# A two-block transformer kernel on one Trainium2 core: inputs by features from the host, a gate's columns on VectorE, eight convolution taps as products on ScalarE

## The chip, the cores and the metric

The kernel runs on one core of one Trainium2 chip. The metric is the device time of one execution, in microseconds (us). The time before is the median of 3 runs, 733.89 us (733.76 to 734.76). A profile is one execution, recorded by the hardware. TensorE (PE; PEld is its weight load) multiplies, VectorE (DVE), ScalarE (ACT) and GpSimd (POOL) work on rows of 128 partitions, SyncE (SP) queues the weight transfers.

## What is computed

Two transformer blocks over 256 positions of 1024 features, in float32, one after the other. Only the first block is touched by the change.

```
silu_c, silu_cc = silu(c), silu(c_ctx)
sh1, sc1, g1, sh2, sc2, g2 = split(silu_c @ w_ada + b_ada)        # and csh1, csc1 for c_ctx
hx = rms_norm(x, norm1_g) * (1 + sc1) + sh1
hc = rms_norm(ctx, norm1_g) * (1 + csc1) + csh1
q, k, v, u = split_proj(hx @ w_in);  kc, vc = hc @ w_in[:, 512:1536]
attn = softmax([rope(q) rope(k)^T / 8 + bias, q kc^T / 8]) [v, vc]   # 8 heads
conv = silu(layer_norm(depthwise_conv(a * sigmoid(b), 31 taps) + bias))
x = x + g1 * ([attn, conv] @ w_out)
x = x + g2 * (square(relu(modulated_norm(x) @ w_mlp1)) @ w_mlp2)
```

## The kernel before

Every engine has a program written out by hand, an instruction queue in fixed order; the engines meet by semaphores (`S[...]`), and a wait stops everything behind it on its engine. A large product is made of three in the type fp32r: each weight unit (1 MB, four or eight blocks of 128 rows) is split by ScalarE into a high half (`WH`, line 1004) and by VectorE into the rest (`WL`, line 1481), each activation likewise (`AH`/`AL`, `CH`/`CL`), and `part` multiplies high by high, high by low, low by high (lines 414 to 416). SP loads the units in the order of `weight_units` into a ring of six slots, each as soon as the unit before it in the slot has been used. The unsplit modulation weights may take either half of a slot.

The stages of the first block, with their place in the profile:

1. Start (0 to 17 us). x arrives by rows. ScalarE sums its squares, GpSimd takes the power -0.5, VectorE scales x (`hat`). TensorE multiplies filler (`keep_busy`, line 476).
2. First loop (to 51 us). For each of eight feature blocks, `mod_first` (line 454) makes 256 columns of shift and scale, as 32 rows in four groups, `mod_turn` turns them to features (line 468) together with the block of scaled x (line 465), VectorE sums and modulates, and `ab` multiplies by the convolution's 1024 input columns (lines 490 to 496).
3. Projections (to 109 us): k, then k and v of the context, q, v. The scaled context is transposed by `c_turn` in the middle of k. VectorE rotates k and q (`rope1`) and adds the taps of the convolution (`taps`, line 1496, one instruction for one tap of one of four channel blocks); ScalarE copies results out of the banks and makes the first tap.
4. Softmax (to 157 us): eight units of two heads and one half of the positions. For each unit TensorE does the scores of the next, half a product of the modulation (`mod_second`, line 433), the tail of the last one (`mod_second_tail`: transposes for shift and scale, for a gate a product with a column of ones, line 621, that spreads the sum to all rows), the values of the unit before (`pv1`, line 598), the other half, and the transposes of the probabilities (`turn1`, line 396). VectorE finds the maxima (`soft1`), scales, and does the remaining taps in between.
5. The output product, the norm, and the feed forward (199 to 340 us) in eight chunks `c`: `up_wide` (lines 731 to 734) and `down1`.

Of the kernel before, what the change touches and what calls it, by code (L numbers as in the profile page):

```python
# [11 lines left out]
D = 1024  # L12
# [12 lines left out]
class Mem:  # L25


    def __init__(self, nc, ctx):
# [42 lines left out]
        self.XC2 = M("XC2", 56, [128, 2, D])  # L71
# [8 lines left out]
        self.cacc = M("cacc", 72, [128, 4, 256])  # L80
        self.ccen = M("ccen", 28, [128, 4, 256])
# [18 lines left out]
        self.combR = M("combR", 84.75, [128, 1], F32R)  # L100
        self.hid = [M(f"hid{i}", 32 + 4 * i, [128, 2, 512]) for i in range(2)]
# [37 lines left out]
l_out w_hi w_lo eps ones silu_c csp hp_zero  # L139
sq_sum mean_sq rstd ada1_mm rows1_dve rows1_turned mod1_sum mod1  # L140
x_hat mx_dve mx_act kx c_hat c_turned mc_dve mc_act kc
a_mm b_mm gate_u u u_turned hp conv_first conv k_mm q_mm v_mm k_out kc_out q_out v_out vc_out rope_mul kr qr qk_turned qk_act
comb_r ada2_mm rows2 rows2_lo rows2_turned mod2_sum mod2
bias_zero scores1 max1 exp1 rl1 p1_norm p1_norm_act p1_turned pt1 pv1
conv_pair conv_block conv_sums conv_dve conv_act conv_rs k_conv a2
out_mm o1_hi o1_lo res1 nscale_dve nscale_act n_turned n_dve n_act kn
m1_mm m1_up m2_mm mlp_sum mlp_act hid_turned hid_hi hid_lo btw
# [3 lines left out]
scores2 max2 exp2 rl2 p2_norm pr2_turned pt2 pv2 g_out g_sig  # L151
y_hi y_lo up_mm merge mrg_turned mrg_hi mrg_lo
out2_mm res2 gu_mm dn_mm silu_g hid2 res3 last_sum x_g y_out y_act""".split()
# [27 lines left out]

OUT_ORDER = [(2, 0), (3, 0), (0, 0), (1, 0), (2, 1), (3, 1), (0, 1), (1, 1)]
# [11 lines left out]
def weight_units(d, S):  # L194
# [27 lines left out]
    for n in range(16):  # L222
        i, half = n // 2, n % 2
        c0 = (3072, 3584, 4096, 4608, 2048, 2560, 5120, 5632)[i]
        add(("ada2", i), "w_ada", 4 * half, 4, [("w_ada", c0, 512)], False, ("ada2_mm", n + 1))
        if n == 7:
            out(2)
            out(3)
        if n == 11:
            out(0)  # L230
            out(1)
# [34 lines left out]
    slots += [2, 12, 3, 13, 4, 14, 5, 15, 0, 1, 2, 12, 3, 13, 4, 5, 2, 12, 3, 13]  # L266
    while len(slots) < len(units):
        slots.append((2, 3, 0, 1, 4, 5)[(len(slots) - 42) % 6])
# [16 lines left out]
def sync_program(e, m, S, units, out, d):  # L285
    w = Waits(e)

# [8 lines left out]
    for tb in range(2):  # L296
        e.dma_start(m.X[:, tb, :], d["x"][128 * tb:128 * tb + 128, :]).then_inc(S[f"l_x{tb}"], 16)
# [3 lines left out]
    for n in range(14, len(units)):  # L301
        load(n)
    for n in range(3):
# [6 lines left out]
def pool_program(e, m, S, d):  # L310
    w = Waits(e)

    def power(i):

        w.wait_ge(S["eps"], 2)
# [18 lines left out]
    e.memset(m.ones[:, :], 1.0).then_inc(S["ones"], 1)  # L334
# [8 lines left out]
    e.memset(m.hp[:, :, 0:15], 0.0).then_inc(S["hp_zero"], 1)  # L343
    e.memset(m.hp[:, :, 271:288], 0.0).then_inc(S["hp_zero"], 1)
# [4 lines left out]
    w.wait_ge(S["eps"], 2)  # L349
# [16 lines left out]
def tensor_program(e, m, S, by):  # L366
# [58 lines left out]
    def mod_unit(unit, k0, bk, sem):  # L425
# [4 lines left out]
        w.wait_ge(S["csp"], 2)  # L430
# [14 lines left out]
    def mod_first(e8):  # L445
# [4 lines left out]
        w.wait_ge(S["csp"], 2)  # L450
# [8 lines left out]
    def mod_turn(e8):  # L459
# [3 lines left out]
        w.wait_ge(S["x_hat"], 2)  # L463
        for tb in range(2):
            e.transpose(bank[b][:, 256 + tb * 128:384 + tb * 128], m.S1[:, tb, 128 * e8:128 * e8 + 128], m.ident[:, :])
# [4 lines left out]
        frees(b, ("mx_dve", e8 + 1))  # L470

    def keep_busy(count):

        w.wait_ge(S["ones"], 1)
# [24 lines left out]
    keep_busy(11)  # L499
    mod_first(0)  # L500
    mod_turn(0)
    keep_busy(8)
    for e8 in range(8):
# [3 lines left out]
        if e8 < 7:  # L507
            mod_turn(e8 + 1)
        ab(e8, 1)
    for tb in range(2):  # L510
        frees(tb, ("u", tb + 1))
        frees(2 + tb, ("gate_u", tb + 1))

    def c_turn(i):
        w.wait_ge(S["c_hat"], 2)
        b = turn(pair(m.XC2, 2 * i), "c_turned")
        frees(b, ("mc_act", 3 * i - 1) if i else ("mc_dve", 2))
# [5 lines left out]

    def c_turns(i):
        c_turn(i)
        c_turn(i + 1)
# [9 lines left out]
    product(by["k"], m.AH, m.AL, 0, 4, "k_mm", x_ready, 512, lambda: c_turns(0))  # L536
    frees(4, ("k_out", 1))
    c_turns(2)
# [23 lines left out]
    qk_turn(m.KR, 2, "kr", 1)  # L562
    qk_turn(m.QR, 3, "qr", 1)
# [46 lines left out]
    def mod_second_tail(i):  # L610
# [6 lines left out]
        else:  # L617
            w.wait_ge(S["comb_r"], 1)
# [1658 lines left out]
```

## Time and profile before

| | us |
|---|---|
| median of 3 runs | 733.89 |
| lowest, highest | 733.76, 734.76 |
| profiled execution, its own time | 736.95 |
| span of its instructions | 735.1 |
| TensorE busy | 722.5 (98%) |
| TensorE weight loads busy | 577.7 (79%) |
| VectorE busy | 508.5 (69%) |
| ScalarE busy | 397.8 (54%) |
| GpSimd busy | 24.9 (3%) |

An instruction's duration runs from its start to its result, and the next one may start before that; so the price of an instruction in a full queue is the step from its start to the start of the next. Busy shares count overlapping instructions once. In the windows below stand, in this order, the stretch and its length, the busy time (and number of instructions) of PE, PEld, DVE, ACT and POOL, TensorE's granted clock as a share of 2.4 GHz, the busy share of the DMA engines, and GB/s; in the timelines the start, the time until the last result, engine, line, operation, output and inputs, and the idle time before it, if any.

### The profile page before, as it was taken

How to read it: one execution, taken by the hardware profiler on the slowest of the kernel's cores; microseconds unless marked ns; L12 is line 12 of the kernel's file. 1: busy time of each engine (PE TensorE's matmuls, PEld its weight loads, DVE VectorE, ACT ScalarE, POOL GpSimd, SP SyncE). 2: the span in 40 equal slices, each digit the busy share in tenths (PEclk: the TensorE clock that was granted, in tenths of full speed). 3: DMA queues.
4: the chain of work that ended last, by engine and by line, in shares of the span. 5: the costliest groups of instructions: out<-in, count | busy, mean ns of one | idle time of the engine just before them, and what ended most of it. 6: DMA issues, size and time to landing. Idle time of an engine off the chain costs nothing.

```text
span 735.1 us, 9749 instructions
## 1 busy us (share of the span) xinstructions
PE 722.5 (98%) x3806; PEld 577.7 (79%) x3806; DVE 508.5 (69%) x924; ACT 397.8 (54%) x662; POOL 24.9 (3%) x44
## 2 busy tenths in 40 slices
PE   7999999999999999999999999999999999999996
PEld 5668885568888888888878777778888888888885
DVE  3688999889667555565988799865857445544544
ACT  3366336886666545556545677666466344434432
POOL 1020011000100000000010000000000000000000
PEclk8999999999999999999999999999999999999999
DMA  9984939954464656545528533344366655655511
GB/s 366 385 325 172 364 114 357 370 171 165 162 221 167 229 182 215 172 157 190 160 96 302 203 116 115 118 171 170 115 230 203 197 173 189 206 177 171 173 58 57
DMA packets 73741, 144.90 MB, mean 197 GB/s; under 512 B 4112, under 2 KB 27664, under 8 KB 72672
## 3 DMA queue, kind: packets, MB, share of 16 engines
q1 hardware_dynamic: 71888, 138.98, 54.6%
q0 software_dynamic: 1520, 5.03, 1.9%
q8 instruction: 30, 0.49, 0.3%
q10 hardware_dynamic: 288, 0.27, 0.1%
q14 instruction: 15, 0.12, 0.0%
HBM read 143.22 MB, written 1.05 MB: 196 GB/s over the span
## 4 chain that ended last, share of the span: by engine, by line
PE 92%; DVE 3%; issue 2%; DMA 1%; ACT 1%; POOL 0%; SPq 0%; POOLq 0%; DVEq 0%
PE bank L414 22%; PE bank L416 22%; PE bank L415 22%; PE bank L734 5%; PE bank L396 5%; PE bank L732 3%; PE bank L433 2%; PE bank L454 1%; DMA W<-in_w_ada 1%; PE bank L576 1%; PE bank L490 1%; PE bank L598 1%; PE bank L851 1%; PE bank L873 1%; DVE WL L1481 1%
## 5 line engine op out<-in xcount | busy, mean ns | idle before, releaser
L1481 DVE TENSOR_TENSOR WL<-W,WH 128x1024 fp32r<-128x1024 f32 (+2 forms) x222 | 249.5, 1169 | 47.7 <-ACT WH L1004 47.4
L1004 ACT ACTIVATE WH<-W 128x1024 fp32r<-128x1024 f32 (+2 forms) x222 | 211.5, 1011 | 52.8 <-DMA W<-in_w_mlp 40.3
L414 PE MATMUL bank<-WH,AHL 128*128 128x512 f32 (+1 forms) x480 | 189.2, 394 | 0.3 <-DVE AHL L1490 0.3
L416 PE MATMUL bank<-WH,AHL 128*128 128x512 f32 (+1 forms) x480 | 185.4, 386 | 0.0
L415 PE MATMUL bank<-WL,AHL 128*128 128x512 f32 (+1 forms) x480 | 185.2, 386 | 0.0
L414 PEld LDWEIGHTS bank<-WH,AHL 128*128 128x128 f32 x480 | 90.2, 188 | 21.5 <-issue 3.2
L416 PEld LDWEIGHTS bank<-WH,AHL 128*128 128x128 f32 x480 | 90.2, 188 | 18.7
L415 PEld LDWEIGHTS bank<-WL,AHL 128*128 128x128 f32 x480 | 90.3, 188 | 16.9
L414 PE MATMUL bank<-WH,HH 128*128 128x512 f32 (+1 forms) x218 | 84.9, 390 | 0.0
L416 PE MATMUL bank<-WH,HL 128*128 128x512 f32 (+1 forms) x218 | 84.5, 388 | 0.0
L415 PE MATMUL bank<-WL,HH 128*128 128x512 f32 (+1 forms) x218 | 84.4, 387 | 0.0
L734 PE MATMUL bank<-AHL,WH 128*128 128x512 f32 x168 | 60.5, 398 | 0.0
L732 PE MATMUL bank<-AHL,WL 128*128 128x256 f32 x192 | 50.0, 281 | 0.0
L1496 DVE SCALAR_TENSOR_TENSOR cacc<-hp,vec,cacc 128x256 f32<-128x256 f32 x120 | 48.3, 475 | 0.0
L416 PEld LDWEIGHTS bank<-WH,HL 128*128 128x128 f32 x218 | 40.9, 188 | 8.5
L415 PEld LDWEIGHTS bank<-WL,HH 128*128 128x128 f32 x218 | 41.0, 188 | 8.3
L414 PEld LDWEIGHTS bank<-WH,HH 128*128 128x128 f32 x218 | 40.9, 188 | 8.0
L1413 ACT ACTIVATE rel<-bank 128x256 f32<-128x256 f32 x22 | 8.5, 384 | 62.2 <-PE bank L416 61.1
L1490 DVE TENSOR_TENSOR hid<-bank,rel 128x256 f32<-128x256 f32 x22 | 9.3, 424 | 42.2 <-ACT rel L1413 42.2
L732 PEld LDWEIGHTS bank<-AHL,WL 128*128 128x128 f32 x192 | 36.3, 189 | 2.0
L734 PEld LDWEIGHTS bank<-AHL,WH 128*128 128x128 f32 x168 | 31.6, 188 | 6.7
L1784 DVE TENSOR_TENSOR HL<-bank,HH 128x256 fp32r<-128x256 f32 (+1 forms) x26 | 11.1, 460 | 30.9 <-ACT HH L1012 30.9
(265 smaller groups left out, 829.5 us busy)
## 6 DMA issues: line engine op xcount, KB each, us to landing
W<-in_w_mlp SPq DMA_DIRECT2D x32, 1024.0 KB, 5.4
W<-in_w_in SPq DMA_DIRECT2D x24, 1024.0 KB, 5.1
W<-in_w_ada SPq DMA_DIRECT2D x12, 1024.0 KB, 7.5
WX<-in_w_ada SPq DMA_DIRECT2D x12, 1024.0 KB, 9.4
W<-in_w_gate SPq DMA_DIRECT2D x22, 512.0 KB, 4.1
W<-in_w_up SPq DMA_DIRECT2D x22, 512.0 KB, 5.3
W<-in_w_down SPq DMA_DIRECT2D x11, 1024.0 KB, 4.9
W<-in_w_out SPq DMA_DIRECT2D x8, 1024.0 KB, 5.0
```

The costliest lines, as they stand in the source:

```text
L396: ins = e.transpose(bank[b][:, c * 128:c * 128 + 128], src, m.ident[:, :])
L414: e.matmul(po, hs, wh[:, k, c0:c0 + cw], start=first and k == 0, stop=False)
L415: e.matmul(po, hs, wl[:, k, c0:c0 + cw], start=False, stop=False)
L416: ins = e.matmul(po, ls, wh[:, k, c0:c0 + cw], start=False, stop=last and k == unit.nk - 1)
L433: ins = e.matmul(bank[bk][32 * g:32 * g + 32, :], m.csp[:, k0 + g, :], wv[:, g, :], start=k0 == 0, stop=k0 == 4, tile_position=(0, 32 * g))
L732: ins = e.matmul(bank[4 + j][:, 0:256], wl[:, k, js], m.AH[:, 4 * i + k, :], start=False, stop=False)
L734: ins = e.matmul(both, wh[:, k, js], m.AHL[:, :, 4 * i + k, :], start=False, stop=i == 1 and k == 3)
L1004: e.activation(m.WH[unit.slot][:, c], m.W32[unit.slot][:, c], ACT.Copy).then_inc(S["w_hi"], 1)
L1481: e.tensor_tensor(m.WL[unit.slot][:, c], m.W32[unit.slot][:, c], m.WH[unit.slot][:, c].bitcast(F32), ALU.subtract).then_inc(S["w_lo"], 1)
L1490: e.tensor_tensor(o, a, b, op).then_inc(S[sem], 1)
L1496: e.scalar_tensor_tensor(o, a, scalar, b, op0, op1).then_inc(S[sem], 1)
L1784: e.tensor_tensor(L[:, k0:k0 + nj, ts], bank[b][:, 0:nj * 128].rearrange("p (j n) -> p j n", j=nj), H[:, k0:k0 + nj, ts].bitcast(F32), ALU ...
```

## The change

- The host also gives x and the context by features (`xt`, `ctxt`). x is no longer scaled and transposed: ScalarE squares it by features, TensorE sums the squares over features with a column of ones (`x_sums`), and the inverse root is spread over all partitions as a row (`spread`), copied to `rB`; VectorE multiplies x by the scale and `rB`, ScalarE adds the shift while it takes the high half, VectorE adds it again while it takes the low one. x by rows is loaded later, for the residual. The context by rows is still loaded for its squares; VectorE multiplies `CT` by the spread root in two instructions; its transposes go.
- The start has 6 + 4 + 4 filler products instead of 11 + 8.
- The gate g2 (columns 5120 to 6144) is no longer a product of the softmax stage. Its weights are loaded to `GW` in the feed forward, in four transfers behind the second unit of `m2` of chunks 2 to 5; VectorE adds them row by row (`gate_rows`, eight instructions of 1024 columns), and TensorE sums over the partitions (`gate_sum`) in chunk 6.
- The last eight of 31 taps: ScalarE multiplies (`tap_products`, 32 instructions of 256 columns), VectorE adds all four channel blocks at once (`add_product`, eight of 1024). VectorE's own taps fall from 120 to 88.
- ScalarE's copy of V to its place waits for the last of these sums, since V shares memory with the products. Some semaphores are merged.

```diff
@@ sync_program
-    for tb in range(2):
-        e.dma_start(m.X[:, tb, :], d["x"][128 * tb:128 * tb + 128, :]).then_inc(S[f"l_x{tb}"], 16)
+    for h in range(2):
+        e.dma_start(m.XT[:, 4 * h:4 * h + 4, :], d["xt"][:, 4 * h:4 * h + 4, :]).then_inc(S[f"l_x{h}"], 16)
...
     for n in range(14, len(units)):
+        if n == 16:
+            e.dma_start(m.CT[:, :, :], d["ctxt"]).then_inc(S["l_ct"], 16)
+        if n == 22:
+            e.dma_start(m.X[:, :, :], d["x"].rearrange("(t p) n -> p t n", p=128)).then_inc(S["l_x"], 16)
         load(n)
+        if n in gate_at:
+            gate_rows(gate_at.index(n))
@@ tensor_program
+    def x_sums():
+
+        for h in range(2):
+            w.wait_ge(S["sq_sum"], h + 1)
+            for k in range(4 * h, 4 * h + 4):
+                for tb in range(2):
+                    ins = e.matmul(bank[6 + tb][:, 0:1], m.xsq[:, k, tb * 128:tb * 128 + 128], m.ones[:, 0:1], start=k == 0,
+                                   stop=k == 7)
+        ins.then_inc(S["r_mm"], 1)
+
+    def spread(b, i):
+
+        w.wait_ge(S["l_id"], 16)
+        w.wait_ge(S["rstd"], i + 2)
+        for tb in range(2):
+            ins = e.matmul(bank[b][:, tb * 128:tb * 128 + 128], m.stat[:, 40 + i + tb:41 + i + tb].to_broadcast([128, 128]),
+                           m.ident[:, :], start=True, stop=True)
+        ins.then_inc(S["r_mm"], 1)
...
-    keep_busy(11)
+    keep_busy(6)
+    x_sums()
+    keep_busy(4)
+    spread(turn_bank("x_spread", 6), 0)
+    frees(6, ("setup", 5))
     mod_first(0)
     mod_turn(0)
-    keep_busy(8)
+    keep_busy(4)
...
-        mod_second(2 * u)
-        if u:
-            mod_second_tail(u - 1)
+        if u < 4:
+            mod_second(2 * u)
+        if u in (1, 2, 3, 4, 6):
+            mod_second_tail(min(u - 1, 4))
...
-        mod_second(2 * u + 1)
+        mod_second(2 * u + 1 if u < 4 else u + 4)
...
+    def gate_sum():
+
+        w.wait_ge(S["comb_r"], 2)
+        w.wait_ge(S["g2_hi"], 1)
+        w.wait_ge(S["g2"], 9)
+        for n in range(2):
...
+            e.matmul(bank[4 + n][:, :], m.onesR[:, :].to_broadcast([128, 128]), m.gH[:, cs], start=True, stop=False)
+            e.matmul(bank[4 + n][:, :], m.onesR[:, :].to_broadcast([128, 128]), m.gL[:, cs], start=False,
+                     stop=True).then_inc(S["g2_mm"], 1)
@@ scalar_program
+    tap_products(0, 1)
     for tb in range(2):
         from_bank("k_mm", 6 + 2 * tb, m.KC[:, tb, :], tb, slice(0, 512), "kc_out")
+        if tb == 0:
+            tap_products(2)
     hi(2)
+    tap_products(3)
     for tb in range(2):
         from_bank("q_mm", 2 + 2 * tb, m.Q[:, tb, :], 2 + tb, slice(0, 512), "q_out", 0.125)
+    tap_products(4, 5)
...
     for tb in range(2):
         from_bank("v_mm", 2 * tb + 2, m.VC[:, tb, :], 4 + tb, slice(0, 512), "vc_out")
+        if tb == 0:
+            tap_products(6, 7)
     qk_features(0, m.kcT)
     qk_features(1, m.qT)
+    w.wait_ge(S["conv_add"], CONV_PRODUCTS)
     from_bank("v_mm", 6, m.V[:, 0, :], 0, slice(0, 512), "v_out")
@@ vector_program
-            hat(m.XC, m.XC2, 0, 2, "c_hat")
-    lo()
-    mean_square(3, (3,))
-    hat(m.XC, m.XC2, 1, 3, "c_hat")
-    lo()
+            mean_square(3, (3,))
+    lo(2)
...
+    for i in range(2):
+        cv = m.CT[:, 4 * i:4 * i + 4, :]
+        rv = bank[m.turn_bank["c_spread", 1]][:, 0:256]
+        tt(cv, cv, rv.unsqueeze(1).to_broadcast([128, 4, 256]), ALU.mult, "c_hat")
     modulate_c0()
...
-    rope1(m.KR, m.Kt, "kr")
-    taps(20)
+    rope1(m.KR, m.Kt, "rotated")
+    taps(8)
+    add_product()
+    add_product()
+    taps(8)
     lo(2)
-    taps(8)
+    add_product()
+    taps(4)
+    add_product()
     w.wait_ge(S["q_out"], 2)
-    w.wait_ge(S["kr"], 1)
-    rope1(m.QR, m.Q, "qr")
-    taps(52)
+    w.wait_ge(S["rotated"], 1)
+    rope1(m.QR, m.Q, "rotated")
+    for n in range(4):
+        taps(6 if n else 2)
+        add_product()
+    taps(16)
...
+        if c < 6:
+            gate_rows(2 * c - 4)
+            gate_rows(2 * c - 3)
+        else:
+            gate_add()
```

## Rows read from the trace of the kernel before

**Rows 1.** The page's head and its first section, TensorE: busy us (share) and instructions

```profile
span 735.1 us, 9749 instructions
...
PE 722.5 (98%) x3806; PEld 577.7 (79%) x3806; DVE 508.5 (69%) x924; ACT 397.8 (54%) x662; POOL 24.9 (3%) x44
```

**Rows 2.** Waits of TensorE: line, waited for: us in total, times, longest

```profile
PE bank L468 <- DVE rows L1521: 0.4, 1, 0.4
...
PE bank L433 <- DVE rows2L L1490: 0.2, 1, 0.2
```

**Rows 3.** Windows: busy us by engine, granted clock, DMA share, GB/s

```profile
9.50:16.00 6.50, 6.42 (x36) 4.78 (x36) 3.00 (x8) 2.72 (x5) 0.00 (x0) 0.51 1.01 419
...
36.00:42.00 6.00, 6.00 (x43) 4.31 (x42) 3.58 (x12) 3.54 (x7) 0.00 (x0) 1.00 0.98 388
120.00:140.00 20.00, 19.97 (x188) 11.08 (x184) 19.75 (x63) 16.72 (x38) 3.02 (x5) 1.00 1.05 379
```

**Rows 4.** Timeline of the start: start, us, engine, line, op, tiles, shape, idle before

```profile
5.42 1.04 ACT L1016 ACTIVATE S<-X 128x1024 f32<-128x1024 f32 x1
...
7.34 0.55 POOL L317 TENSOR_TENSOR stat<-stat 128x1 f32<-128x1 f32 x1 [0.93 <-DVE stat L1507]
7.93 0.75 DVE L1493 TENSOR_SCALAR S<-X,stat 128x1024 f32<-128x1024 f32 x1 [0.67 <-POOL stat L317]
...
9.57 1.94 PE L454 MATMUL bank<-W,csp 128*32 128x256 f32 x16 [2.72 <-DMA W<-in_w_ada]
...
12.53 3.56 PE L476 MATMUL bank<-ones 128*128 128x128 f32 x16
...
15.04 0.42 DVE L1490 TENSOR_TENSOR AHL<-S,AHL 128x256 fp32r<-128x256 f32 x1
...
17.02 0.73 PE L490 MATMUL bank<-WH,AHL 128*128 128x512 f32 x2
```

**Rows 5.** Timeline of the softmax stage, units 6 and 7

```profile
148.97 0.49 DVE L1493 TENSOR_SCALAR s<-s,rl 128x512 f32<-128x512 f32 x1
...
149.72 1.06 PE L433 MATMUL bank<-WX,csp 128*32 128x512 f32 x8
...
150.71 1.34 PE L396 MATMUL bank<-ident,s 128*128 128x128 f32 x8
...
152.05 1.07 ACT L1012 ACTIVATE PT<-bank 128x512 f32<-128x512 f32 x2
...
155.90 0.61 PE L639 MATMUL bank<-ones,csum 128*128 128x1 f32 x4
...
156.37 1.07 PE L396 MATMUL bank<-ident,s 128*128 128x128 f32 x8
```

**Rows 6.** Timeline of TensorE around the first transposes of the context

```profile
53.45 0.39 PE L416 MATMUL bank<-WH,AHL 128*128 128x512 f32 x1
53.68 1.03 PE L396 MATMUL bank<-ident,XC 128*128 128x128 f32 x8
...
54.79 0.39 PE L415 MATMUL bank<-WL,AHL 128*128 128x512 f32 x1
```

**Rows 7.** Timelines of ScalarE and of VectorE, projections of the first block

```profile
47.76 3.89 ACT L1004 ACTIVATE WH<-W 128x1024 fp32r<-128x1024 f32 x4
...
66.81 2.08 ACT L1075 ACTIVATE cacc<-hp,vec 128x256 f32<-128x256 f32 x4
...
106.63 1.16 ACT L1012 ACTIVATE qrT<-bank 128x512 f32<-128x512 f32 x2
...
62.19 4.63 DVE L1481 TENSOR_TENSOR WL<-W,WH 128x1024 fp32r<-128x1024 f32 x4 [0.26 <-ACT WH L1004]
...
90.88 20.68 DVE L1496 SCALAR_TENSOR_TENSOR cacc<-hp,vec,cacc 128x256 f32<-128x256 f32 x52
```

**Rows 8.** Timeline of TensorE, the first scores

```profile
108.98 0.70 PE L576 MATMUL bank<-kT,qrT 64*128 64x256 f32 x4
```

**Rows 9.** Timeline of VectorE in the first feed forward, between two chunks

```profile
245.40 2.36 DVE L1481 TENSOR_TENSOR WL<-W,WH 128x1024 fp32r<-128x1024 f32 x2 [7.28 <-ACT WH L1004]
```

## What I expect of the change

> **What bounds the kernel now.** Read the page first: TensorE is busy for 98% of the span [rows 1]. Then its waits: beside the start-up filler and the first weights (2.72 us, at 9.57 [rows 4]) the longest is 0.4 us, for a copy of modulation rows, and one of 0.2 stands in the softmax [rows 2]. So the end is set by TensorE's queue, and what leaves that queue should come off the span unless a wait takes its place. Whether one does is read from the windows: in 36 to 42 us the DMA engines are full (0.98, 388 GB/s), and in 120 to 140 us VectorE is busy 19.75 of 20 us and ScalarE 16.72 [rows 3]. TensorE does not wait there, but VectorE has nothing to spare, so a TensorE that gets ahead will meet VectorE. Three stretches matter: the start (0 to 17 us), the projections of the first block (51 to 112), its softmax (112 to 157). The first feed forward (199 to 340) gets new work.
>
> **Start.** Removed: 2 transposes and 5 of 19 filler products. Added ahead of the first modulation product: 16 row-sum products of one column, two short scalar steps on VectorE, two powers on GpSimd, and 2 products that spread the result. Before, the powers went through VectorE beside the filler and cost TensorE nothing; the first product waited for weights until 9.57 [rows 4]. No row shows 16 one-column products; the nearest is the pair in the softmax stage, 0.47 us from its start to the next start (155.90 to 156.37), so 0.235 each at full clock [rows 5]. The squares end at 5.4 and 6.4 (the second starts at 5.42 and takes 1.04 [rows 4]), so the sums run from 5.5 to 5.5 + 16 x 0.235 = 9.3. Then 0.5 for two scalar steps and handovers, 2 x 0.55 for the powers, so the spread starts near 11.1. It is two products of 128 columns like the filler's, 3.56 / 8 = 0.44 each at the clock of that stretch [rows 4]: 0.9. The first modulation product thus starts at about 12.0 instead of 9.57: 2.4 later. Given back: four filler products fewer behind it, 1.8, and two transposes, 0.3. The start ends some 0.3 late (ready data would allow no better: from 9.57 to the first full operand is 15.46 - 9.57 = 5.9 us, which ends at 17.9, and the low half of the operand is needed half way through the first tile). The bounds are the clock's: the granted clock of 9.5 to 16 us is 0.51, that is 1.2 GHz, and 1.00 after [rows 3]; the engine rose again after 3.56 us of filler without a gap. If it stays at 1.2 GHz through the first tile, the start is some 3.5 late; if it never falls, 1.5 early.
>
> **First loop.** 8 transposes in a row cost 0.88: the next product comes 54.79 - 53.68 - 0.23 us after the place where it would have been (0.23 is the step between products, 53.45 to 53.68), so 0.11 each [rows 6]. 14 transposes of x in the loop: 1.54. The 0.4 wait of the rows copy and 0.15 beside it also go, since the context's scaling that held VectorE is gone: 0.55. The 16 transposes of the context: 1.76, against one spread of 0.5 (0.44 x 2 at half the clock, so half of it here, and a change of form). Sum at the end of the k product: 1.54 + 0.55 + 1.76 - 0.5 = 3.3 early.
>
> **Projections: where it is given back.** The feature-wise context is one more MB, queued ahead of the two k units while the DMA engines are full; at 388 GB/s that is 2.7 us [rows 3]. The k units then reach ScalarE about when they did (their split began at 47.76 [rows 7], would be ready 2.1 sooner by TensorE, and lands 1.2 too late for that), however early TensorE is. Two context scalings of 1024 columns on VectorE follow, 2 x 1.14 (four steps of that size and form took 4.63, the last 1.22 of it alone [rows 7]), where two of 0.75 [rows 4] stood, in part earlier, so VectorE starts the q halves near 62.7, not 62.19. From there to its first row maximum, behind 52 taps that end at 111.5, it took 49.3 us, 0.8 of it waits. New: 24 taps fewer in this stretch (80 to 56) at 20.68 / 52 = 0.397, -9.5; 8 sums of 1.14, +9.1; each sum must wait for the end of the step before it and holds the step after, so it loses the overlap of 0.08 twice, 0.2 a sum with the handover, +1.6; the waits, less 0.2, go. 62.7 + 49.3 - 0.6 - 9.5 + 9.1 + 1.6 = 112.6 against 111.49. So the eight taps moved save VectorE nothing before the softmax. ScalarE's 32 products (0.52 each, 2.08 / 4 [rows 7]) hide in idle time between its copies, one each 5.5 us. But its copy of V now waits for the last sum, which stands 16 taps (6.4 us) ahead of the row maximum, at 106.3; behind it queue five copies of some 0.53 (1.16 for two [rows 7]), so the first scores go at 109.0, where TensorE would have been ready at 108.98 - 3.3 = 105.7 [rows 8]. The 3.3 us are gone, and since the row maximum is 1.1 late, TensorE enters the softmax loop up to 0.9 late. The sums are not in the trace: between a one-operand step of that size, 0.75 [rows 4], which would give 3.1 back, and 1.22 with nothing overlapped, which takes 0.6. I take 1.14, the row with their form and operands.
>
> **Softmax.** Removed: 4 half products of the modulation (149.72 to 150.71, 0.99 each) and 2 tails of two products of 512 columns (2 x 0.23 and a change of form, 0.6), 5.2 [rows 5]. One new wait: with these gone, the values product of unit 6 comes right behind the transposes. From the scaling of that unit on VectorE (148.97) to the end of the two copies that it needs (152.05 + 1.07) is 4.15 us [rows 5], over two maxima and two exponentials, less 0.5 for a rows copy that goes: 3.65. TensorE has only 0.6 + 1.0 of work in it, so it waits 2.0. A wait of 0.2 goes [rows 2]. Net 5.2 - 2.0 + 0.2 = 3.4, less the 0.9: 2.5 early, up to 3.3. VectorE's share falls (28 taps in the loop, not 36) and does not bind here.
>
> A rule speaks against this term. LDWEIGHTS are busy 11.08 of 20 us in this stage while matmuls fill it [rows 3]. The Trainium skill (Perfetto Trace Analysis, Identifying the Most-Contended Engine) says to judge TensorE's headroom by LDWEIGHTS busy share, not by matmul busy time. By that rule TensorE is not the bound here and the 5.2 us bring nothing; that is a rival below. I follow the starts, which stand back to back.
>
> **First feed forward.** Added: 4 products of 512 columns with two switches, 4 x 0.23 + 0.1 = 1.0 on TensorE, nothing beside it. On VectorE 8 row steps of 1.14 to 1.2, two a chunk: they stand where it idles 7.28 us for ScalarE [rows 9]; were the cover gone, each pair would cost 2.4, four times. The 4 MB that left the softmax stage come here, each behind a weight load on SP with the next one not yet free. ScalarE's copy of the sum stands in the same idle time. Nothing else.
>
> **Sum.** 2.5 (to 3.3) - 1.0 = 1.5 to 2.3, taken as 1.8. The profiled execution took 736.95 us (span 735.1), 3 above the median 733.89; it would become 735.1. On the median: 732.1.
>
> **Rivals.**
> 1. Forecast: VectorE and the loads take the first gain, 732.1. Chance 0.45.
> 2. TensorE keeps it all: its queue is 98% of the span, and my lateness of VectorE hangs on 1.1 us. Then 3.3 + 5.4 - 1.0 = 7.7, 726.2; half of it, 729. Chance 0.17. Against: the 19.75 of 20.
> 3. The clock stays at 1.2 GHz into the first tile, since the row sums are short and the filler is cut: 3.5 late at the start; 1.5 of that hides, since the k units land 1.2 after they are wanted and the start was counted 0.3 late already, so 1.8 - 2.0 = -0.2, 734.1. Chance 0.18.
> 4. Slower: the row sums themselves run at 1.2 GHz, 0.44 rather than 0.235 each, +3.3 on top of rival 3, at 5.5 to 13 us. Start 5.5 to 7 late: 736 to 737. It decides from a start 4.8 late (1.5 hidden, 1.8 gain, 1.5 for 0.2%). Chance 0.13.
> 5. The rule on LDWEIGHTS: the 5.2 bring nothing, 733.9 - 1.8 + 3.4 = 735.5. Chance 0.07.
>
> About 0.2%, 1.5 us, can be told from no change. Faster: rival 2 and two thirds of the forecast's, 0.47. Same: the rest of the forecast's and most of rival 3, 0.33. Slower: rivals 4 and 5, 0.20. The range 728.5 to 736.0 leaves out the full rival 2 and most of 4.
>
> **What will show it.** Start: the first modulation product at about 12, the first tile at 17 to 18 with a granted clock of 1.00 behind it. Loop: a step of 4.19 instead of 4.41. Projections: a TensorE wait of some 3 us ahead of the first scores, released by ScalarE; VectorE's first row maximum at 112 to 113. Softmax: a wait of 2 us ahead of one values product at about 148 to 150, by ScalarE. Feed forward: no TensorE wait. I am wrong if the first scores come without a wait, or if the first tile starts past 20 us.

## The result and the profile after

The changed kernel takes 739.72 us (739.60 to 740.23, median of 4 runs), the kernel before in the same comparison 733.86 (733.76 to 734.76, 4 runs): 1.0075 of it, 95% interval 1.0062 to 1.0088. It is 5.9 us slower. The forecast was 732.1 with a range up to 736.0; the direction was wrong.

The first lines of the page of after, which answer to [rows 1] (busy us, share of the span, number of instructions):

```profile
span 738.4 us, 9708 instructions
## 1 busy us (share of the span) xinstructions
PE 723.0 (98%) x3772; PEld 580.2 (79%) x3772; DVE 515.5 (70%) x907; ACT 411.0 (56%) x691; POOL 24.6 (3%) x44
```

TensorE is as full as it was, in a span 3.3 us longer. Its waits in after (us in total, times, longest), against [rows 2]:

```profile
PE bank L617 <- ACT qrT L1069: 2.7, 1, 2.7
PE bank L423 <- DVE g1b L1572: 0.9, 1, 0.9
PE bank L639 <- ACT PT L1069: 0.7, 1, 0.7
```

The waits foretold ahead of the first scores (L617) and of a values product (L639) are there. The loss is elsewhere. TensorE's timeline of after from its first instruction to its first tile (a product of this type leaves two records, so x32 is 16 products):

```profile
2.76 2.93 PE L500 MATMUL bank<-ones 128*128 128x128 f32 x12 [2.76 <-POOL ones L361]
6.21 6.99 PE L529 MATMUL bank<-ones,xsq 128*128 128x1 f32 x32 [0.52 <-ACT xsq L1105]
13.06 2.06 PE L500 MATMUL bank<-ones 128*128 128x128 f32 x8
14.90 1.07 PE L538 MATMUL bank<-ident,stat 128*128 128x128 f32 x4
15.90 1.94 PE L481 MATMUL bank<-W,csp 128*32 128x256 f32 x16
18.48 0.41 PE L492 MATMUL bank<-ident,rows 128*128 128x128 f32 x2 [0.64 <-DVE rows L1603]
18.72 1.06 PE L500 MATMUL bank<-ones 128*128 128x128 f32 x8
19.71 1.07 PE L481 MATMUL bank<-WX,csp 128*32 128x256 f32 x16
20.71 0.50 PE L514 MATMUL bank<-WH,AHL 128*128 128x512 f32 x1
```

From the first of the 16 row sums to the product behind them it takes 13.06 - 6.21 = 6.85 us, 0.428 each, not 0.235. The four filler products behind them still take 2.06 us, and the first modulation product 1.94; only from 18.7 on do the same forms take 1.06 and 1.07. The first tile starts at 20.71, 3.7 us behind the 17.02 of [rows 4].

And 17.02 was itself no normal start. A second profiled execution of the kernel before, unchanged (its own time 734.04 us, its span 732.2), has these rows in TensorE's timeline:

```profile
2.76 4.92 PE L476 MATMUL bank<-ones 128*128 128x128 f32 x22 [2.76 <-POOL ones L334]
8.95 1.07 PE L454 MATMUL bank<-W,csp 128*32 128x256 f32 x16 [1.27 <-DMA W<-in_w_ada]
...
10.84 1.95 PE L476 MATMUL bank<-ones 128*128 128x128 f32 x16
...
13.72 0.73 PE L490 MATMUL bank<-WH,AHL 128*128 128x512 f32 x2
```

Here the first modulation product already takes 1.07 us and the first tile starts at 13.72. Two of the kernels below that begin with the same instructions have it at 13.59 and 14.34 in their records. So against a usual execution of before, after starts its first tile 7.0 us late. The 3 us by which the first record of before exceeded its median lay in that start (17.02 - 13.72 = 3.3).

The stages, read from single rows of VectorE in the two records (end of the taps and first row maximum, then the step that ends the softmax's modulation). Second record of before:

```profile
108.53 0.69 DVE L1666 CUSTOM_DVE_ANT_0 s<-bias,bank 128x512 f32<-128x512 f32 x1
...
156.60 0.16 DVE L1496 SCALAR_TENSOR_TENSOR A<-mod,vec 128x8 f32<-128x8 f32 x1
```

After, the same with the halves of the q unit ahead:

```profile
66.62 3.50 DVE L1563 TENSOR_TENSOR WL<-W,WH 128x1024 fp32r<-128x1024 f32 x3 [0.26 <-ACT WH L1061]
...
116.88 0.68 DVE L1774 CUSTOM_DVE_ANT_0 s<-bias,bank 128x512 f32<-128x512 f32 x1
...
161.67 0.16 DVE L1578 SCALAR_TENSOR_TENSOR A<-mod,vec 128x8 f32<-128x8 f32 x1
```

| after against the second record of before | us late |
|---|---|
| first tile (20.71 against 13.72) | 7.0 |
| first row maximum (116.88 against 108.53) | 8.4 |
| end of the softmax's modulation (161.67 against 156.60) | 5.1 |
| end of the span (738.4 against 732.2) | 6.2 |

The softmax gave 3.3 back and the feed forward cost 1.1, both near the forecast. The start alone is later (7.0) than all that was given back behind it (2.0 in the first loop, 3.3 in the softmax).

### The profile page after: what moved, and what is told of

Read it like the earlier page. It is cut to its first block, busy times and chain, and to the rows that moved or that the text cites. A ratio compares the mean times of both kernels' runs of the same rounds, so it can differ in the third digit from the quotient of the medians.

```text
span 738.4 us, 9708 instructions
## 1 busy us (share of the span) xinstructions
PE 723.0 (98%) x3772; PEld 580.2 (79%) x3772; DVE 515.5 (70%) x907; ACT 411.0 (56%) x691; POOL 24.6 (3%) x44
## 4 chain that ended last, share of the span: by engine, by line
PE 84%; DVE 8%; ACT 4%; issue 2%; DMA 2%; POOL 0%; POOLq 0%; DVEq 0%; SPq 0%
PE bank L441 20%; PE bank L443 20%; PE bank L442 20%; PE bank L776 5%; PE bank L423 4%; PE bank L774 3%; DVE cacc L1578 2%; DVE WL L1563 1%; PE bank L460 1%; PE bank L481 1%; DVE cacc L1572 1%; ACT WH L1061 1%; DMA W<-in_w_in 1%; PE bank L617 1%; PE bank L529 1%
## 5 line engine op out<-in xcount | busy, mean ns | idle before, releaser
L443 PEld LDWEIGHTS bank<-WH,AHL 128*128 128x128 f32 x480 | 90.4, 188 | 18.7
L1578 DVE SCALAR_TENSOR_TENSOR cacc<-hp,vec,cacc 128x256 f32<-128x256 f32 x88 | 36.0, 479 | 0.2
```

The lines of the kernel that those rows point to most:

```text
L443: ins = e.matmul(po, ls, wh[:, k, c0:c0 + cw], start=False, stop=last and k == unit.nk - 1)
L1578: e.scalar_tensor_tensor(o, a, scalar, b, op0, op1).then_inc(S[sem], 1)
```

## The experiments

Two theories were set against each other. S: the loss is made at the start, by the row sums on TensorE. V: it is made by VectorE and the loads ahead of the softmax, behind which the start would be hidden. Most kernels with row sums on TensorE scatter more from one execution to the next (by up to 6.5 us within one kernel, as 734.66 to 741.17) than those with x by rows (by at most 3.6), so their records are read with their times.

**The kernel before again.**

> The kernel before, unchanged, to see a second profiled execution of it. Its first one took 736.95 us, 3.1 above the median, and its filler products ran at half the later pace until 15.5 us. Theory A, that this execution was an odd one at its start: the second profile shows 733.9 us, the filler at the higher pace sooner, and the first tile some 3 us before 17.02. Theory B, that the start is always like this and the 3.1 us lie elsewhere: the first tile again at 17.0.

Measured: 734.08 us (733.83 to 734.92); first tile at 13.72, its record's own time 734.04. Theory A holds.

**x by rows.**

```diff
+        for tb in range(2):
+            e.transpose(bank[b][:, 256 + tb * 128:384 + tb * 128], m.S1[:, tb, 128 * e8:128 * e8 + 128], m.ident[:, :])
...
-    keep_busy(6)
-    x_sums()
-    keep_busy(4)
-    spread(turn_bank("x_spread", 6), 0)
-    frees(6, ("setup", 5))
+    keep_busy(11)
     mod_first(0)
     mod_turn(0)
-    keep_busy(4)
+    keep_busy(8)
```

> The kernel after with one part undone: x is loaded, scaled and transposed by rows as in the kernel before, with 11 and 8 filler products; context by features, gate on VectorE and tap products stay. Theory S (the loss is the 16 row-sum products, 6.99 us on TensorE ahead of the first modulation product): the first tile is back at 17.0 or earlier, against 20.71, and the time falls by 3.7 to 6, from 739.7 to 733.7 to 736.0, although 14 transposes (1.5 us) come back. Theory V (the loss is made later, by VectorE and the loads ahead of the k units, and hides the start): the halves of the q unit on VectorE stay at 66.6, its first row maximum at 116.9, and the time stays within 739.0 to 740.5.

Measured: 734.41 us (733.85 to 736.19), 1.0001 of before (0.9992 to 1.0011). The start of TensorE in its record:

```profile
8.76 1.93 PE L479 MATMUL bank<-W,csp 128*32 128x256 f32 x16 [0.93 <-DMA W<-in_w_ada]
...
14.91 0.73 PE L515 MATMUL bank<-WH,AHL 128*128 128x512 f32 x2
```

and VectorE's halves of the q unit:

```profile
61.12 4.63 DVE L1550 TENSOR_TENSOR WL<-W,WH 128x1024 fp32r<-128x1024 f32 x4 [0.26 <-ACT WH L1048]
```

The first tile is 5.8 us earlier than in after, VectorE's q halves 5.5, the time 5.3. Theory S holds: nearly the whole loss is x by features, and little hides it. It also says that the other three parts together bring nothing.

**Taps on VectorE.**

```diff
-CONV_PRODUCTS = 8
+CONV_PRODUCTS = 0
...
-    for n in range(4):
-        taps(6 if n else 2)
-        add_product()
-    taps(16)
+    taps(52)
...
-        taps((8, 7, 7, 6, 0, 0, 0, 0)[u])
+        taps((9, 8, 8, 7, 4, 0, 0, 0)[u])
```

> The kernel after with one part undone: all taps but the first on VectorE, one instruction each, as in the kernel before (80 ahead of the first row maximum, 36 behind); V's copy then waits for no sum. Theory S: this part is worth little ahead of the softmax (eight sums for 24 taps, +1.0 in the record of the kernel after) and 8 taps, 3.2 us, in it, where VectorE is nearly full: first row maximum 1.0 earlier, 115.9, softmax up to 3.2 longer, time 740 to 742. Theory V (the sums and V's copy behind them are the loss): the time falls by 2 to 4, to 736 to 738, and the wait of 2.7 us ahead of the first scores goes.

Measured: 739.09 us (734.48 to 740.88, 6 runs), between the two forecasts. In its record, which is that of its slowest execution (740.88 us, first tile at 22.62), a TensorE wait of 2.1 us for VectorE's scaling stands in the softmax in place of the 2.7 ahead of the scores. The part moves a wait; the 0.6 us between the medians is less than this kernel scatters. The run with an undisturbed start below gives its size.

**The gate in the softmax.**

```diff
-        if u < 4:
-            mod_second(2 * u)
-        if u in (1, 2, 3, 4, 6):
-            mod_second_tail(min(u - 1, 4))
+        mod_second(2 * u)
+        if u:
+            mod_second_tail(u - 1)
...
-        if c == 6:
-            gate_sum()
```

> The kernel after with one part undone: the gate's columns are a product of the softmax stage again, as in the kernel before, and the feed forward has no row steps and no sum. If TensorE's starts bind in the softmax: +5.2 us there, less 0.7 (the wait ahead of a values product), less 1.0 of the sum in the feed forward: 739.7 + 3.5 = 743.2. If the rule on weight loads were right and these products cost nothing in that stage: 739.7 - 1.0 = 738.7.

Measured: 741.81 us (738.15 to 744.65). In its record, from the first row maximum to the end of the softmax's modulation:

```profile
116.53 0.68 DVE L1766 CUSTOM_DVE_ANT_0 s<-bias,bank 128x512 f32<-128x512 f32 x1
...
164.91 0.17 DVE L1869 COPY modB<-mod 128x8 f32<-128x8 f32 x1
```

That is 48.4 us. The row of the same copy in after is

```profile
161.75 0.17 DVE L1876 COPY modB<-mod 128x8 f32<-128x8 f32 x1
```

so after has 161.75 - 116.88 = 44.9: 3.5 us for the gate's products in the softmax, less about 1 in the feed forward. The medians are 2.1 us apart. The gate part helps.

**More filler ahead of the row sums.** `keep_busy(6)` becomes `keep_busy(11)`.

> The kernel after with one number changed: 11 filler products ahead of the row sums instead of 6. In the second record of the kernel before, 11 products took 4.92 us and everything behind ran at the higher pace; after six (2.93 us) the row sums took 0.437 each, and the filler behind them 0.5 still. Theory P (the row sums cost 0.437 because TensorE is at its lower pace, and they do not raise it): with 11 the sums start at 7.7 at the higher pace, take 16 x 0.235 = 3.8 and end at 11.5 instead of 13.1; all behind runs at the higher pace, first tile near 16.5 instead of 20.7, time 735.5 to 736.5. Theory W (each such product costs 0.437 by its own work, a load of 128 columns for one column of result): they end at 14.7, the first tile is at 19 to 22, time 738.5 to 741.5.

Measured: 740.44 us (737.49 to 741.72), no faster. TensorE's rows:

```profile
7.22 4.12 PE L529 MATMUL bank<-ones,xsq 128*128 128x1 f32 x32
11.20 2.06 PE L500 MATMUL bank<-ones 128*128 128x128 f32 x8
...
20.64 0.73 PE L514 MATMUL bank<-WH,AHL 128*128 128x512 f32 x2
```

and windows of the same record, the first three within the sums:

```profile
9.50:10.00 0.50, 0.50 (x7) 0.50 (x6) 0.00 (x0) 0.00 (x0) 0.00 (x0) 1.00 1.10 459
10.00:10.50 0.50, 0.50 (x5) 0.50 (x5) 0.00 (x0) 0.00 (x0) 0.00 (x0) 0.69 1.06 442
10.50:11.00 0.50, 0.50 (x4) 0.50 (x4) 0.00 (x0) 0.13 (x1) 0.00 (x0) 0.50 1.01 426
...
9.00:13.00 4.00, 4.00 (x25) 4.00 (x25) 0.23 (x2) 1.15 (x2) 1.08 (x2) 0.65 1.01 423
13.00:20.00 7.00, 6.36 (x44) 4.11 (x46) 3.43 (x9) 1.55 (x3) 0.00 (x0) 0.50 1.02 422
```

Theory P was half right. The sums began at the higher pace and followed each other every 0.223 us. But at 10.2, with 13 to 14 of the 16 done, the granted clock fell to 0.50 of 2.4 GHz, 1.2 GHz, although TensorE had been busy without a gap since 2.75 and still was. The last sums and nearly all behind them, up to the first tile, ran at the lower pace, and the first tile starts where it did. So the sums cost in two ways, by their own time and by the pace of all that follows them. Theory W is out: at the higher pace a sum takes half of what it takes at the lower.

**Row sums of 128 columns.** More work, same weight loads:

```diff
-                    ins = e.matmul(bank[6 + tb][:, 0:1], m.xsq[:, k, tb * 128:tb * 128 + 128], m.ones[:, 0:1], start=k == 0,
+                    ins = e.matmul(bank[6 + tb][:, 0:128], m.xsq[:, k, tb * 128:tb * 128 + 128], m.ones[:, :], start=k == 0,
```

> The kernel after with one thing changed: each of the 16 row-sum products has 128 columns instead of one (the moving operand is the whole block of ones, so every column is the same sum). The weight loads are the same, and so is their number; there is more work, not less. Theory C (products of one column let TensorE's pace stay at or fall to the lower level): with 128 columns the pace rises within the sums, from 0.49 to 0.265 each; they end near 11.5 instead of 13.06, all behind at the higher pace, first tile near 16.5 instead of 20.7, time 735 to 736.5. Rival (the pace follows when the engine was busy at all, or the loads of weights, and the width is no matter): sums at 0.437 to 0.5 each, end at 13 to 14.2, first tile at 20.7 or later, time 739.5 to 741.

Measured: 737.54 us (734.92 to 739.31), 2.2 less than after. The record is that of its fastest execution (734.92 us).

```profile
6.09 4.81 PE L529 MATMUL bank<-ones,xsq 128*128 128x128 f32 x32 [0.41 <-ACT xsq L1105]
...
13.10 1.07 PE L481 MATMUL bank<-W,csp 128*32 128x256 f32 x16
...
17.04 0.73 PE L514 MATMUL bank<-WH,AHL 128*128 128x512 f32 x2
```

Sixteen products with 128 times the columns end 2.3 us sooner (10.9 against 13.2), because the pace rises within them (at 8.2), and all behind them runs at the higher one. Where the slower executions of this kernel lose their time no record shows.

**Both.** The last two edits together, so that only the width differs from the one with 11 filler products.

> The kernel after with 11 filler products ahead of the row sums and 128 columns in each of these. It differs from the one with 11 filler products by the width of the sums alone; there the clock was granted at 0.65 over 9 to 13 us and 0.50 from 13 to 20, and the time was 740.4. Theory C (products of one column make the pace fall or stay low): sums of 0.265 to 0.3 each from 7.4 to 11.8, the granted clock stays 1.00, first tile at 17 to 18, time 735.5 to 737. Rival (the longer filler or the waits behind the sums make it fall): granted 0.5 again from 11 or 13 on, first tile at 20 to 21, time 740.

Measured: 736.45 us (735.36 to 739.37), against 740.44 with one column. The granted clock stays where it was:

```profile
7.05 3.74 PE L529 MATMUL bank<-ones,xsq 128*128 128x128 f32 x32
...
16.92 0.73 PE L514 MATMUL bank<-WH,AHL 128*128 128x512 f32 x2
...
9.00:13.00 4.00, 3.31 (x32) 3.03 (x31) 0.22 (x2) 1.15 (x2) 1.09 (x2) 1.00 1.02 425
13.00:20.00 7.00, 6.36 (x57) 4.23 (x56) 4.80 (x15) 1.57 (x4) 0.00 (x0) 1.00 1.02 420
```

The two kernels differ by the width of the sums alone. The longer filler is no cause, since both have it, and the waits behind the sums are none, since in the other kernel the clock fell before them, within the sums. From the first sum to the product behind the last it takes 10.62 - 7.05 = 3.57 us here, 0.223 each, the step of the one-column sums at the higher pace too: the 128 columns cost nothing of their own. This is shown for these two widths, by one record of each and by the medians of 12 and 6 runs, and for nothing between.

**Squares added first.** VectorE adds the eight blocks of squares to one, TensorE has two sums behind 12 filler products.

```diff
+    for i, (a, b, n) in enumerate(((0, 2, 2), (4, 6, 2), (0, 4, 2), (0, 1, 1))):
...
+        tt(flat(m.xsq[:, a:a + n, :]), flat(m.xsq[:, a:a + n, :]), flat(m.xsq[:, b:b + n, :]), ALU.add, "setup")
```

> The kernel after, with the squares added on VectorE to one block first (four steps, 1024 columns at most 0.6 each by those of 512 and 1024 read so far), so that TensorE has 2 row-sum products instead of 16, behind 12 filler products instead of 6. Theory S (the start is the loss): the sums end near 9.5 instead of 13.06, the first tile comes near 15.5 instead of 20.7, and the time falls by some 5, to 734 to 735.5. Theory V (the rest of the change hides the start): 738.5 to 740.

Measured: 735.89 us (734.66 to 741.17); first tile at 17.10, later than expected, since the granted clock fell to 0.68 over 9 to 13 us, behind a wait of 1.5.

**The modulation ahead of the spread.**

```diff
-    keep_busy(4)
-    spread(turn_bank("x_spread", 6), 0)
...
     mod_first(0)
     mod_turn(0)
+    spread(turn_bank("x_spread", 7), 0)
```

> As the one with the squares added, and the first modulation product, its turn and VectorE's small steps on it stand ahead of the spread and of the copy of the spread, which need the power. TensorE then waits for the first weights (8.8 to 9) as in the kernel before, and the spread hides beside VectorE's steps. Theory S: first tile at 13.5 to 14.5, as in the second record of the kernel before (13.72), and what is left is the loop (14 transposes, 1.5 us, gone), the softmax (+3.3) and the gate (-1.0) against the projections (-1.4 or more): 731.5 to 733.5. Theory V: no better than with x by rows, 734.4.

Measured: 735.82 us (735.30 to 737.17). The first tile is 1.45 earlier than in the one before, at 15.65, the time no better: the forecast missed. ScalarE's rows in it and in the next kernel say why. It waits for the k units:

```profile
46.54 2.01 ACT L1060 ACTIVATE WH<-W 128x1024 fp32r<-128x1024 f32 x2 [1.81 <-DMA W<-in_w_in]
49.25 2.01 ACT L1060 ACTIVATE WH<-W 128x1024 fp32r<-128x1024 f32 x2 [0.70 <-DMA W<-in_w_in]
```

**The context's load behind the k units.**

```diff
-        if n == 16:
+        if n == 18:
             e.dma_start(m.CT[:, :, :], d["ctxt"]).then_inc(S["l_ct"], 16)
```

> As the one with the modulation first, but the context by features is queued behind the two k units instead of ahead of them. There the first tile came at 15.65, 1.45 before that of the one with the squares added only (17.10), and yet the context's scaling on VectorE came no sooner (53.8 and 53.5), behind k units that ScalarE awaited. Theory D (the extra MB ahead of the k units is what the start's gain runs into): the k units land up to 2.7 earlier, the context's scaling starts at 51 to 52, the first row maximum at 110.5 to 111.5 instead of 113.1, time 733.5 to 734.3. Rival: VectorE's own work in that stretch binds, and the order of the loads changes nothing, 735.8.

Measured: 733.29 us (732.77 to 734.59), 0.9988 of before (0.9979 to 0.9996), 2.5 less than with the load ahead. The context's scaling starts at 52.49 instead of 53.82, the first row maximum at 111.19 instead of 112.53. ScalarE goes through the four halves without a wait, although this execution's first tile came at 17.00:

```profile
45.67 3.93 ACT L1060 ACTIVATE WH<-W 128x1024 fp32r<-128x1024 f32 x4
```

Theory D holds, and with it a part of theory V: one more MB in front of the k units has its price, once the start is in order.

**The same with x by rows.** Both edits, the one of x by rows and the one of this load.

> The kernel after with x by rows, and the context by features loaded behind the two k units instead of ahead of them. Against the kernel with x by rows (734.4) it moves the load alone; with context by rows too, it was 732.2. If the extra MB ahead of the k units is the price of context by features: time 732.5 to 733, halves of the q unit on VectorE at 60.0 instead of 61.1, their distance from the first tile less by as much. If VectorE's two scalings of 1024 columns (2.34 us for both) are the price: 734.1 to 734.5.

Measured: 733.65 us (732.05 to 735.49), 0.8 below 734.41 and between the two forecasts. From the first tile to VectorE's q halves it takes 60.76 - 15.41 = 45.35 us, with the load ahead 61.12 - 14.91 = 46.21. Against context by rows (732.18, below) some 1.5 us are left over, which goes with VectorE's two scalings (2.34 us) and the first tile 1.07 us later in that record (15.41 against 14.34); these were not separated.

**V copied later.**

```diff
-    w.wait_ge(S["conv_add"], CONV_PRODUCTS)
-    from_bank("v_mm", 6, m.V[:, 0, :], 0, slice(0, 512), "v_out")
     qk_features(2, m.kT)
     qk_features(3, m.qrT)
+    w.wait_ge(S["conv_add"], CONV_PRODUCTS)
+    from_bank("v_mm", 6, m.V[:, 0, :], 0, slice(0, 512), "v_out")
```

> The kernel after with ScalarE's copy of V, and its wait for the last sum, moved behind the copies of the features of k and q. It tells what the wait of 2.7 us ahead of the first scores is worth. If it is a loss of its own: scores at 110.5 instead of 113.1, time 737 to 738. If VectorE binds there (first row maximum at 116.9, behind 16 taps): scores come earlier, the row maximum stays within 0.3 of 116.9, a wait of the same size moves behind it, and the time stays at 739.2 to 740.

Measured: 739.03 us (735.19 to 741.57). The scores came at 110.51 instead of 113.15, the first row maximum at 116.12 instead of 116.88 (its first tile was 0.5 earlier too), and a wait of 2.1 us for VectorE's scaling stood in the softmax. The wait ahead of the scores is VectorE's lateness in another place. 0.7 us lie within this kernel's scatter, so a small price of its own is not excluded.

**The gate alone, on the kernel before.** Of the change, only `gate_rows`, `gate_sum` and the shorter softmax queue are left.

> The kernel before with one part of the change alone: the gate's columns on VectorE in the first feed forward. x and context by rows, all taps but the first on VectorE. Undoing the gate in the kernel after cost 2.1 us (741.8 against 739.7). If the softmax gives the same here: from VectorE's first row maximum to the end of the softmax 44.9 us as with the taps on VectorE, instead of 47.55 in the second record of before, less 1.0 in the feed forward: 1.6 faster, 732.4 against 734.1. If VectorE's 36 taps in that stage take it all back (19.75 of 20 us busy [rows 3]): 734.1 + 1.0 = 735.1.

Measured: 733.03 us (732.10 to 735.67), 0.9984 of before (0.9973 to 0.9996): 1.2 faster by the medians of this comparison (before 734.22), 1.6 by the spans of the two records (730.6 against 732.2). 1.6 was expected.

**The gate and the tap products, on the kernel before.** `tap_products` and `add_product` too.

> The kernel before with the gate on VectorE and the eight taps as products on ScalarE with their eight sums; x and context by rows. Against the one with the gate alone it gives the price of the tap products with an undisturbed start. By the records of after and of the one with the taps on VectorE: +1.7 ahead of the first row maximum (50.87 against 49.2 from the halves of q), -0.6 in the softmax (44.3 against 44.9): 1.1 slower than the gate alone, 733.5. If the taps in the softmax are what holds that stage up: 0.5 to 1 faster than the gate alone, 731.5.

Measured: 732.18 us (731.67 to 733.21), 0.9974 of before (0.9965 to 0.9983), the best of all, 2.0 below before and 0.85 below the gate alone, a step whose intervals overlap. VectorE's rows of its record:

```profile
60.06 4.63 DVE L1544 TENSOR_TENSOR WL<-W,WH 128x1024 fp32r<-128x1024 f32 x4 [0.26 <-ACT WH L1042]
...
110.34 0.69 DVE L1749 CUSTOM_DVE_ANT_0 s<-bias,bank 128x512 f32<-128x512 f32 x1
...
154.42 0.16 DVE L1559 SCALAR_TENSOR_TENSOR A<-mod,vec 128x8 f32<-128x8 f32 x1
```

50.3 us to the first row maximum and 44.1 from there to the end of the modulation; the gate alone has 49.3 (59.27 to 108.56) and 45.5 (to 154.02). The taps cost 1.0 ahead of the softmax and give 1.4 in it. The expected loss was wrong: I had taken the cost ahead of the softmax from the record of an execution with the first tile at 22.62, and the gain in it from the record of after, in whose softmax a fall of the clock cost 0.7 us (see below under projections).

## Why the prediction was wrong

**The start, two steps.** First, the price of the row sums. I took 0.235 us each from a pair in the softmax stage [rows 5], at full clock, though the rows of the start itself show filler at 0.44 a product [rows 4] and a granted clock of 0.51 [rows 3]. Measured: 0.428 at the lower pace, 0.223 at the higher; so the price was right for full clock, and the clock was wrong. The sums were to take 3.8 us, to 9.3; they took 6.85 from 6.21, and the first modulation product came at 15.90 instead of 12.0. That the clock stays low behind short row sums was rival 3, that the sums themselves run low, at 0.44, rival 4 (0.13). What no rival held is that the clock falls within such sums once it has risen, as in the run with 11 filler products. Second, the reference. I saw that the profiled execution was 3 us above the median and took the 3 us as spread evenly, by forming the difference in the record and subtracting it from the median. They were in the stretch that the change rebuilds. Against a first tile at 13.72, my own estimate of the start (0.3 later than 17.02) would have been 3.6 us late, and the sum 1.8 - 3.3 = 1.5 slower, 735.4. The second error alone turned the sign. The kernel with 11 filler products and sums of 128 columns bears this out: with its first tile at 16.92, close to my 17.3, it took 736.45, some 2.2 more than before in the same comparison (734.22), and 3.3 less than after. So each of the two errors is worth about 3 us.

**First loop.** Right. A step is 4.18 us (products at 40.75 and 44.93), 4.19 was foretold. The product behind the loop stands 5.0 us late (53.02 against 48.02) where the first tile was 7.0 late: 2.0 given back, of 1.54 + 0.55.

**Projections.** Right in kind. From the q halves to the first row maximum 50.3 us against 49.3 in the second record of before: 1.0 more; I had 49.9, 0.6 more. The wait ahead of the first scores was 2.66, released by ScalarE (3.3 foretold). Behind it the clock fell: over 113 to 117 us it was granted at 0.62 and 0.52.

```profile
113.00:115.00 2.00, 1.85 (x9) 1.10 (x9) 2.00 (x7) 1.38 (x2) 0.00 (x0) 0.62 0.97 376
115.00:117.00 2.00, 2.00 (x5) 1.61 (x6) 2.00 (x6) 0.00 (x0) 0.00 (x0) 0.52 0.05 12
```

In the record of the row sums of 128 columns the same wait (2.6 us) stands without such a fall, with

```profile
112.45 0.68 DVE L1774 CUSTOM_DVE_ANT_0 s<-bias,bank 128x512 f32<-128x512 f32 x1
...
156.52 0.16 DVE L1578 SCALAR_TENSOR_TENSOR A<-mod,vec 128x8 f32<-128x8 f32 x1
```

From the scores to the first row maximum it is 3.7 us in both, so the fall does not delay VectorE there. But from that maximum to the end of the modulation it is 44.1 us here and 44.8 in after. Of the other kernels with the same work in the softmax, six with the fall there have 44.7 to 44.8, one in which it lasted longer 46.0, and two without it 44.1. So the fall cost 0.7 us, which I had not counted. The load of the context was costed at 2.7 us and then said to leave the k units where they were; moved alone it was worth 2.5 us with x by features (and the squares added on VectorE) and 0.8 with x by rows.

**Softmax.** The number was right, 3.3 us against 3.4, with some luck: the waits were 0.7 at the values product and 0.9 at a transpose held by VectorE's addition to the first gate, 1.6 in place of 2.0, and the fall of the clock took 0.7 back. The Trainium skill (Perfetto Trace Analysis, Identifying the Most-Contended Engine) judges TensorE's headroom by LDWEIGHTS busy share and by the share of peak arithmetic reached. My reading of it, that products taken out while LDWEIGHTS are busy half of the time would bring nothing, does not hold in this stage: with the gate put back it was 3.5 us longer.

**Feed forward.** Right: 5.1 late becomes 6.2, 1.1 for the 1.0 that was counted. The row steps on VectorE took 1.28 (1.14 to 1.2 foretold), in idle time.

**The rivals.** The full gain (rival 2) did not come, and rival 5 was wrong, since the gate's 5.2 us did bring something. The mechanism of rivals 3 and 4 did, with the price of rival 4; in the record of after the clock rose at 17.9, ahead of the first tile, so not for as long as rival 3 said. Against the 17.02 from which they were counted the start was 3.7 us late, not rival 4's 5.5 to 7. By its own sum (1.5 hidden, 1.8 gain) a start 3.7 late makes 0.4 slower, 734.3. That the time lies beyond its 736 to 737 comes from the odd reference, so rival 4's number was founded no better than mine. I had also named the sign: a first tile past 20 us.

## What to carry to other kernels

Before a stretch is costed, ask whether the profiled execution is the median one, and if not, where its surplus lies: a surplus in the very stretch that changes belongs in the sum. Take a price from the stretch where the new instructions will run, at the pace that TensorE has there, and look at what a change puts in front of the products that bring it to its full pace. A gain that survives alone (here the gate and the taps, 2 us) is worth having without the part that was to go with it.

## What the runs showed of the hardware

- At either pace a float32 product of one column with weights of its own costs TensorE what one of 128 columns costs. From start to start it is 0.428 us at the lower pace (16 one-column sums of after) and 0.223 at the higher (the first sums of the kernel with 11 filler products); filler of 128 columns has 0.427 and the sums of 128 columns 0.223.
- TensorE, busy without a gap for 6.85 us on products of one column, did not rise from the lower pace. In the four records of kernels with 6 filler products and these 16 sums it rose between 16.7 and 22.6 us. With sums of 128 columns in their place it rose at 8.2, and in ten of the eleven records of kernels with 11 or 12 filler products at the head between 5.7 and 8.5 (12.4 in the eleventh, with x by rows). In one kernel the clock fell at 10.2, within such one-column sums and without a gap since 2.75; with 128 columns in their place it did not. The Trainium skill (TensorE: Matmul & The Clock Gate, The HAM clock gate) says that the warm-up is a matter of time and not of a number of products. For filler of 128 columns the runs agree in so far as they show no fixed number (7 to 11 products before the rise, where it fell within the filler), though in one record 11 brought none. For 6.85 us of products of one column they do not agree.
- The granted clock of the trace is no guide before its first change, which stands at 17.9 in after. It reads 1.00 over 9 to 20 us there, where the same four filler products take 2.06 us at 13.06 and 1.06 at 18.72. The step from product to product tells the pace:

```profile
9.00:13.00 4.00, 4.00 (x20) 4.00 (x21) 0.00 (x0) 1.15 (x2) 0.00 (x0) 1.00 1.01 422
13.00:20.00 7.00, 6.36 (x47) 4.62 (x51) 2.05 (x9) 0.00 (x0) 1.08 (x2) 1.00 1.02 421
```

The Trainium skill (TensorE: Matmul & The Clock Gate, Seeing it yourself) warns that the clock's events in a trace can be unreliable. This case shows a narrower thing: the share is not to be read ahead of the first event.
- Behind the wait of 2.6 to 2.7 us ahead of the first scores the granted clock fell to 0.50 in seven records (in after from 113.5 to 116.9 us) and not in an eighth. With the fall the same softmax stage took 44.8 us, without it 44.1.
